# A hybrid decoder trunk on one Trainium2 core: per-head decay sums from one product per head, and three lists reordered

## The reference

```python
acs = jnp.cumsum((dt * a_neg).reshape(bsz, nc, L, ng, ne), axis=2)
ah = jnp.transpose(acs, (0, 1, 3, 4, 2))
decay = jnp.exp(jnp.where(causal, ah[..., :, None] - ah[..., None, :], -jnp.inf))
cb = jnp.einsum('bctgn,bcsgn->bcgts', cc, bc)
y_intra = jnp.einsum('bcgts,bcgets,bcsgep->bctgep', cb, decay.astype(x.dtype), xw)
w_end = jnp.exp(ah[..., -1:] - ah).astype(x.dtype)
st_loc = jnp.einsum('bcges,bcsgn,bcsgep->bcgepn', w_end, bc, xw)
y_inter = (jnp.einsum('bctgn,bcgepn->bctgep', cc, s_start.astype(x.dtype))
           * jnp.exp(acs)[..., None].astype(x.dtype))
```

## Time and profile before

| what | value |
|---|---|
| median of 3 executions | 1561.26 us (1561.2 to 1562.8) |
| profiled execution, its own time | 1561.38 us |
| its span in the trace | 1559.6 us |
| TensorE busy | 1538.0 us, 99% |
| VectorE busy | 1073.6 us, 69% |
| ScalarE busy | 809.2 us, 52% |
| GpSimd busy | 153.5 us, 10% |
| granted TensorE clock | 0.999 of full |
| HBM traffic | 173 GB/s over the span |

### The profile page before, as it was taken

How to read it: one execution, slowest core, us unless ns; L and a number is a source line. 1 busy time by engine, 2 the same in 40 slices (tenths; PEclk the granted TensorE clock), 3 DMA queues, 4 the chain that set the end, 5 groups by cost and what they waited for, 6 DMA issues and landing times.

```text
span 1559.6 us, 28133 instructions
## 1 busy us (share of the span) xinstructions
PE 1538.0 (99%) x11594; PEld 1439.7 (92%) x11594; DVE 1073.6 (69%) x1314; ACT 809.2 (52%) x1141; POOL 153.5 (10%) x147
## 2 busy tenths in 40 slices
PE   7999999999999999999999999999999999999998
PEld 6999999999999979999899999998999999799996
DVE  5556578889887546565765556799888866555556
ACT  6444385664655355443564445755766633544444
POOL 1000011233130000000000000113243100000001
PEclk9999999999999999999999999999999999999999
DMA  8665554456455556655565555454544465466551
GB/s 253 195 198 192 175 158 110 146 153 186 135 157 190 193 168 204 200 188 190 166 192 192 194 196 165 123 156 136 188 134 152 153 206 197 149 211 195 199 189 69
DMA packets 245089, 271.09 MB, mean 174 GB/s; under 512 B 12560, under 2 KB 226152, under 8 KB 245012
## 3 DMA queue, kind: packets, MB, share of 16 engines
q1 hardware_dynamic: 239504, 266.90, 53.6%
q10 hardware_dynamic: 5364, 2.98, 0.7%
q0 software_dynamic: 144, 0.15, 0.0%
HBM read 268.94 MB, written 1.05 MB: 173 GB/s over the span
## 4 chain that ended last, share of the span: by engine, by line
PE 90%; DVE 4%; issue 3%; ACT 2%; DMA 1%; SPq 0%; POOL 0%; ACTq 0%; POOLq 0%; DVEq 0%
PE bank L1562 29%; PE bank L1646 28%; PE bank L1592 8%; PE bank L1593 8%; PE bank L1594 8%; PE bank L1995 1%; PE bank L1587 1%; PE bank L1850 1%; DVE w_lo L936 1%; PE bank L1578 1%; PE bank L1580 1%; PE bank L1579 1%; ACT w_hi L530 1%; DVE xcv L1174 1%; DMA w_raw<-in_w_ffn_dram 1%
## 5 line engine op out<-in xcount | busy, mean ns | idle before, releaser
L936 DVE TENSOR_TENSOR w_lo<-w_raw,w_hi 128x2048 fp32r<-128x2048 f32 x248 | 576.9, 2328 | 315.8 <-ACT w_hi L530 315.5
L530 ACT ACTIVATE w_hi<-w_raw 128x2048 fp32r<-128x2048 f32 x248 | 474.1, 1916 | 307.4 <-PE bank L1646 131.0
L1646 PE MATMUL bank<-f_lo,w_hi 128*128 128x256 f32 x1280 | 355.6, 278 | 0.0
L1646 PE MATMUL bank<-f_hi,w_lo 128*128 128x256 f32 x1280 | 353.5, 276 | 0.0
L1646 PE MATMUL bank<-f_hi,w_hi 128*128 128x256 f32 x1240 | 342.6, 276 | 0.0
L1562 PE MATMUL bank<-u_hi,w_hi 128*128 128x256 f32 x1152 | 326.6, 283 | 1.3 <-DVE w_lo L936 1.3
L1562 PE MATMUL bank<-u_lo,w_hi 128*128 128x256 f32 x1152 | 319.9, 278 | 0.0
L1562 PE MATMUL bank<-u_hi,w_lo 128*128 128x256 f32 x1152 | 319.9, 278 | 0.0
L1646 PEld LDWEIGHTS bank<-f_hi,w_lo 128*128 128x128 f32 x1280 | 240.4, 188 | 0.0
L1646 PEld LDWEIGHTS bank<-f_lo,w_hi 128*128 128x128 f32 x1280 | 240.4, 188 | 0.0
L1646 PEld LDWEIGHTS bank<-f_hi,w_hi 128*128 128x128 f32 x1240 | 232.8, 188 | 0.0
(11 more groups left out here) (308 smaller groups left out, 2453.8 us busy)
## 6 DMA issues: line engine op xcount, KB each, us to landing
w_raw<-in_w_ffn_dram SPq DMA_DIRECT2D x262, 512.0 KB, 4.3
w_raw<-in_w_in_dram SPq DMA_DIRECT2D x160, 512.0 KB, 4.9
w_raw<-in_w_branch_b_dram SPq DMA_DIRECT2D x32, 512.0 KB, 4.4
w_raw<-in_w_branch_a_dram SPq DMA_DIRECT2D x16, 512.0 KB, 4.5
w_raw<-in_w_out_dram SPq DMA_DIRECT2D x16, 512.0 KB, 4.1
w_raw<-in_w_ple_gate_dram SPq DMA_DIRECT2D x16, 512.0 KB, 4.3
y_feat<-in_w_ple_dram ACTq DMA_DIRECT2D x2, 1024.0 KB, 4.9
h<-in_x_dram SPq DMA_DIRECT2D x2, 512.0 KB, 5.5
```

The lines of the kernel that those rows point to most:

```text
L530: a_.activation(whi[slot][:, :, :], raw[slot][:, :, :], ACT.Copy).then_inc(sem["w_hi"], 1)
L936: v_.tensor_tensor(wlo[slot][:, :, :], raw[slot][:, :, :], whi[slot][:, :, :].bitcast(F32), ALU.subtract).then_inc(sem["w_lo"], 1)
L1646: i = mm(o, four(w[slot])[:, k, cs], x[:, rows0 + k, :], start=opens, stop=(not start and k == 3 and q == 2), skip_group_check=True)
```

## The change

Once a layer, when dA is there, VectorE writes its hi and lo parts into `twin`, zeroed matrices with 40 columns per chunk and group that hold the group's 8 heads twice, at columns 0 and 32. TensorE multiplies them with the triangle `tri_le_r`: 16 products of 40 by 128, so that the running sums acs of every head stand as rows, twice, in partitions 0 to 7 and 32 to 39 of banks 4 and 5. ScalarE copies them rounded into the tile `acs` (`sums_high`), VectorE replaces rows 32 to 39 by what the rounding left (`sums_low`). Another product gives acs as columns (`acol`). `segments` and `from_start` are gone. A head's row is put on all partitions by one product of 128 by 256 with `pick`, a matrix that has ones in the two rows of that head (`sums(half)`, four products, twice a group). ScalarE then takes, per head and chunk, Relu(acol - row) and the exponential of minus that, four heads and two chunks at once, and the exponential of the row for cs. The building of R_hi and R_lo is gone. POOL clears `acs` and `twin` and makes `pick` once a layer. The order of VectorE's list changes at several places too, in group 0 and in the loop, and ScalarE's with it.

```diff
+                g_.memset(acs[:, :, :].bitcast(F32), 0.0)
...
+                    i = g_.memset(twin[b][:, :, :, :].bitcast(F32), 0.0)
...
+                    i = g_.tensor_tensor(pick[b][:, :, :], ident[:, e].unsqueeze(2).broadcast_to([P, EH // 2, P]),
+                                         ident[:, f].unsqueeze(2).broadcast_to([P, EH // 2, P]), ALU.add)
...
-                    def distances_of(g, c, half):
-                        part_of(R_hi, dA_hi, g, c, half)
-                        part_of(R_lo, dA_lo, g, c, half).then_inc(sem["r_built"], 1)
+                    def sums_high():
+
+                        act.wait_ge(sem["acs_done"], lay + 1)
+                        for b in range(2):
+                            i = a_.activation(acs[0:40, 2 * b:2 * b + 2, :],
+                                              bank[4 + b][0:40, :].rearrange("p (g s) -> p g s", g=2), ACT.Copy)
+                        i.then_inc(sem["acs_hi"], 1)
...
+                    def decay(half):
+
+                        act.wait_ge(sem["seg_done"], G * 2 + (half + 1))
+                        for e in range(4 * half, 4 * half + 4):
+                            for c in range(NC):
+                                i = a_.activation(seg[:, c, e, :], bank[4 + e // 2][:, (e % 2) * S + c * P:(e % 2) * S + (c + 1) * P],
+                                                  ACT.Relu, scale=-1.0, bias=acol[:, c, bass.ds(g * EH + e, 1)])
+                        i.then_inc(sem["gap_ready"], 1)
+                        for e in range(4 * half, 4 * half + 4, 2):
+                            a_.activation(cs[:, e:e + 2, :], two(4 + e // 2)[:, :, P:2 * P], ACT.Exp)
+                        act.wait_ge(sem["gap_ready"], G * 2 + (half + 1))
+                        a_.activation(seg[:, :, 4 * half:4 * half + 4, :], seg[:, :, 4 * half:4 * half + 4, :],
+                                      ACT.Exp, scale=-1.0).then_inc(sem["exp_done"], 1)
...
+                pe.wait_ge(sem["dA_split"], lay + 1)
+                for g in range(NG):
+                    for c in range(NC):
+                        o = bank[4 + g // 2][0:40, (g % 2) * S + c * P:(g % 2) * S + (c + 1) * P]
+                        mm(o, twin[0][:, c, g, :], tri_le_r[:, :], start=True, stop=False)
+                        i = mm(o, twin[1][:, c, g, :], tri_le_r[:, :], start=False, stop=True)
+                i.then_inc(sem["acs_done"], 1)
...
-                    def segments(c, half):
...
-                    def from_start():
...
+                        for e in range(4):
+                            i = mm(bank[4 + 2 * half + e // 2][:, (e % 2) * S:(e % 2 + 1) * S], pick[half][:, e, :],
+                                   acs[:, bass.ds(g, 1), :].rearrange("p a b -> p (a b)"), start=True, stop=True)
+                        i.then_inc(sem["seg_done"], 1)
...
-                        conv(2, 0, (4, 5), xcv[:, 2:4, :])
-                        silu(2, xcv[:, 2:4, :])
-                        mask_cb()
+                        conv(2, 0, (4, 5), xcv[:, 2:4, :])
+                        mask_cb()
+                        silu(2, xcv[:, 2:4, :])
```

More of the change, by code:

```diff
@@ L112, in trunk @@
         top[0] = place(feat_at, 512, 1024)
+        ha_hi_at = top[0]
         ha_hi = sb("ha_hi", [P, 2 * MH, S], F32R)
+        ha_lo_at = top[0]
         ha_lo = sb("ha_lo", [P, 2 * MH, S], F32R)
+        last_group = 2 * (MH - 1) * S * 4
+        pick = [at(f"pick{b}", [P, EH // 2, P], F32R, off + last_group)[0] for b, off in enumerate((ha_hi_at, ha_lo_at))]
         top[0] = place(top[0], 512, 1024)
@@ L186, in trunk @@
         late = a
-        xwe_at = late + NC * EH * HP * 4
+        twin = [at(f"twin{b}", [P, NC, NG, 40], F32R, late + b * 40 * NC * NG * 4)[0] for b in range(2)]
         xw, a = at("xw", [P, NC, EH * HP], F32, a)
@@ L800, in body @@
                         step(9)
[L801 to L805, removed]
-                        act.wait_ge(sem["y_done"], G + 1)
-                        for half in range(2):
-                            part_of(R_lo, dA_lo, g + 1, 0, half).then_inc(sem["r_built"], 1)
                     act.wait_ge(sem["ha32_ready"], G + 1)
@@ L1108, in softplus_gates, with sums_low @@
                 dve.wait_ge(sem["dA_ready"], lay + 1)
-                ch.add(v_.tensor_copy(dA_hi[:, :, :], dA[:, :, :]))
+                dve.wait_ge(sem["twin_clear"], lay + 1)
+                by_group = dA[:, :, :].rearrange("p c (g e) -> p c g e", g=NG)
+                for r in (0, 32):
+                    ch.add(v_.tensor_copy(twin[0][:, :, :, r:r + EH], by_group))
                 ch.wait()
-                v_.tensor_tensor(dA_lo[:, :, :], dA[:, :, :], dA_hi[:, :, :].bitcast(F32), ALU.subtract)\
-                    .then_inc(sem["dA_split"], 1)
+                for r in (0, 32):
+                    i = v_.tensor_tensor(twin[1][:, :, :, r:r + EH], by_group, twin[0][:, :, :, r:r + EH].bitcast(F32),
+                                         ALU.subtract)
+                i.then_inc(sem["dA_split"], 1)
+            def sums_low(lay):
+                dve.wait_ge(sem["acs_hi"], lay + 1)
+                for b in range(2):
+                    o = acs[32:40, 2 * b:2 * b + 2, :]
+                    i = v_.tensor_tensor(o, bank[4 + b][32:40, :].rearrange("p (g s) -> p g s", g=2), o.bitcast(F32),
+                                         ALU.subtract)
+                i.then_inc(sem["acs_ready"], 1)
             def gate_rows(lay):
@@ L1290, in body @@
                         gate_rows(lay)
+                        sums_low(lay)
                         step(3)
@@ L1880, in body @@
                         pe.wait_ge(sem["tok_ready"], lay * 2 + 2)
-                        segments(1, 0)
-                        segments(1, 1)
-                        unit(Z0, lambda *a: feat(*a, between=from_start))
+                        sums(0)
+                        unit(Z0, lambda *a: feat(*a, between=lambda: sums(1)))
                         cb()
@@ L1899, in body @@
                         unit(BC, feat)
-                        unit(QK, lambda *a: feat(*a, between=lambda: segments(0, 0)))
-                        segments(0, 1)
-                        unit(X01, lambda *a: feat(*a, between=lambda: segments(1, 0)))
-                        segments(1, 1)
+                        unit(QK, lambda *a: feat(*a, between=lambda: sums(0)))
+                        unit(X01, lambda *a: feat(*a, between=lambda: sums(1)))
                         evac(QK)
@@ L1906, in body @@
                         unit(X23, feat)
-                        unit(V, lambda *a: tok(*a, between=from_start))
+                        unit(V, tok)
                         cb()
```

107 lines of the change are left out of this document (47 added, 60 removed).

## The result

The changed kernel takes **1580.86 us** (median of four, 1578.81 to 1581.81) against 1561.47 for the kernel before (four runs): a ratio of 1.012, 95% interval 1.0105 to 1.0135. It is slower by 19.4 us. I had said 1570 with a range up to 1574: the side was right, the size less than half of what came. The profiled execution took 1580.18 us, its span is 1578.4, and the granted clock is 0.994 of full, against 0.999 before.

A forecast was written before the change was run, and what follows sets the result against it. TensorE was busy all the time, VectorE's loop list within 1% of it. With w_lo late, 61.4 us a group puts Z1 of group 3 4.3 us later, 8.6 over two layers: 1561.3 + 8.6 = 1569.9, said 1570; range 1553 to 1574.

The forecast's parts named there:

- Products, 12.8 us: TensorE, per layer: old products worth 22.3 us go, new ones cost 7.4 and 2.1; ends 10.9 and 14.9.
- ScalarE: A decay takes 3.7 us, costing nothing in the loop; in group 0 silu(1) starts at 247.5 instead of 246.94.
- Group 0: End of group 0 on VectorE: hrms stands behind a w_lo, so L1362 starts at 276.0, 2.1 us later.
- C: End of the third convolution's last step in a group, on VectorE; in group 1 forecast 1.6 us later, at 306.7.
- VectorE's own period, 59.8 us: VectorE's time per loop group, 60.9 us before, less 1.1 us from moving w_lo and the mask earlier.
- The port: Loop, SBUF access: POOL's seg starts before silu(2), which is slowed; the w_lo of Z1 ends at C + 7.7.
- The sum: Loop groups take 61.4 us: 33.3, 10.3, 10.05 and 7.8; Z1 of group 3 comes 4.3 us later per layer.
- Z1's start to the end of the next QK: TensorE stretch of the loop, first term of the group time: 32.3 us before, forecast 33.3.
- the two rings: Loop dependency chain from Z1's start through QK, convolutions and w_lo to the next Z1, forecast at 61.4 us per group.
- TensorE stays the bound: Rival: all 12.8 us of saved products come through, perhaps 1.4 us of waits too; 1547 to 1550 us, chance 0.12.
- VectorE gets the port for silu(2) and the w_lo: Rival: VectorE runs both in one go, Z1 of group 3 comes 3.0 us earlier; 1555 us, chance 0.18.
- The race of the third: Rival: silu(2) starts before POOL's first seg, but the w_lo stands behind that seg; 1559.5 us, chance 0.20.

The follow-up runs named there:

- experiments 1: Changed kernel with silu(2) put back ahead of mask_cb in the loop: 1561.45 us, ratio 0.9994 to the kernel before.
- experiment 5: Changed kernel with silu(2) back ahead of mask_cb and the old end of group 0 in VectorE's list: 1557.72 us, ratio 0.9975.
- experiment 7: Changed kernel with VectorE's list in the old order everywhere, keeping the new sums and ScalarE's changed order: 1556.09 us, ratio 0.9966.
- experiment 2: Changed kernel, mask still ahead of silu(2), but GpSimd's first seg step waits for that silu: 1558.76 us, ratio 0.9978.
- experiment 4: Changed kernel with 20 extra 256-column products on TensorE ahead of Z1 in groups 1 to 3 of each layer: 1573.84 us, ratio 1.0075.
- number 10: Changed kernel with VectorE's old order except mask_cb ahead of silu(2), and GpSimd held until that silu is done: 1554.04 us, ratio 0.9949.
- experiment 9: Changed kernel with GpSimd's first seg step held until silu(2) is done and the old end of group 0: 1555.46 us, ratio 0.996.
- experiment 8: Kernel before with one edit, mask_cb ahead of silu(2) in the loop: 1586.35 us, ratio 1.0161.
- experiment 6: Changed kernel with the loop order silu(2), w_lo of Z1, mask_cb, and the old end of group 0: 1567.12 us, ratio 1.0031.

## Why the prediction came out wrong

**Products, 12.8 us.** The twin products take what I gave them, about 0.06 us each; TensorE's timeline of the changed kernel:

```profile
224.02 0.22 PE L1771 MATMUL bank<-tri_le_r,twin 128*40 128x128 f32 x1
224.08 0.22 PE L1772 MATMUL bank<-tri_le_r,twin 128*40 128x128 f32 x1
```

The Trainium skill (TensorE: Matmul & The Clock Gate, Back-to-back issue gap) has about 81 ns for a steady product of 128 columns; here, with 40 columns of weights, it is 60. Comparing the starts of TensorE's units in the two traces, a loop group is shorter by 1.6 us over the units BC to V, where I had 1.86, and group 0 by 0.9 and 1.0. That makes 11.5 us in all; by the distances between the starts of the old and the new products alone it is 12.5. Both are between my ends of 10.9 and 14.9. Right.

**ScalarE.** silu(1) of group 0 at 247.05; I had 247.5, and a decay at 3.7 (the first of group 0 runs from 237.17 to 240.83). Right.

**Group 0.** L1373 at 275.55, forecast 276.0; hrms behind the w_lo, as said. Right, and the price too: C of group 1 at 306.22, forecast 306.7. Not seen: TensorE itself waits 2.1 us there for gate_a. Here that is swallowed by the later wait for w_lo; it shows once that one is gone (experiments 1 and 5).

**VectorE's own period, 59.8 us.** Not confirmed. With the port out of the way (experiment 5) Z1 comes after 59.7 and 59.8 us in the first layer, but TensorE has no wait there from Z1 of group 1 to Z1 of group 3, so this is TensorE's own pace: the 61.3 us from group 2 to group 3 before, in which it did not wait either, less the 1.6 us of products. That the number is mine is luck; it shows only that VectorE needs no more. And the mask, whose early place was 0.35 us of my sum, stands late in that run. The old order has 60.4 and 60.5 (experiment 7) and is not slower: what the moves gain per group they lose once in group 1, whose Z1 starts at 310.54 in experiment 5 and at 309.04 in experiment 7.

**The port.** POOL first, silu 2.6 (2.73), the w_lo of Z1 done at C + 7.7 (7.8), Z1 of group 1 at 314.5 (314.14). Right in every step, and experiment 2 shows it as the cause. The trace agrees once more with the exclusive lock of the Trainium skill (SBUF — State Buffer, Who interferes with whom).

**The sum: the step that failed.** "61.4 us per group". In the changed kernel it took 64.8 and 63.8 from one Z1 to the next. The failed term is its first, "Z1's start to the end of the next QK", which I took from the trace before and so at Z1's old pace: what a lower clock behind the new wait costs was put at nothing. VectorE's rows on the way from Z1 of group 1 to Z1 of group 2:

```profile
349.90 0.42 DVE L1230 SCALAR_TENSOR_TENSOR qT<-bank,rB 128x256 f32<-128x256 f32 x1 [1.11 <-PE bank L1572]
...
357.97 2.29 DVE L933 TENSOR_TENSOR w_lo<-w_raw,w_hi 128x2048 fp32r<-128x2048 f32 x1 [0.39 <-ACT w_hi L540]
...
360.90 0.74 DVE L1182 TENSOR_SCALAR xcv<-xin,gcw,gcb 128x256 f32<-128x256 f32 x2
...
368.25 2.71 DVE L1185 SCALAR_TENSOR_TENSOR xcv<-xin,gcw,xcv 128x256 f32<-128x256 f32 x6
```

From Z1 at 314.14 to the evacuation of QK at 349.90 it is 35.76 us where I had 33.3. Z1 itself is 2.4 longer than the 5.5 of before, and that is the difference. From there to the convolution of X01 it is 11.00 instead of 10.3, for hand-overs that I had left out (0.39 ahead of the w_lo at 357.97, for its w_hi). Then 10.06 to C, as forecast, and C + 7.96. From group 2 to group 3 the first two are 34.82 (Z1 1.65 longer) and 11.07. So Z1 of group 3 came at 442.75 instead of 437.3. Of the 5.8 us that the two rings were longer than forecast, about 4 are Z1's slow products, 3.6 of them the clock's if one counts from the 5.75 us of an undisturbed Z1 behind a wait; the rest are mostly the hand-overs. The first layer lost 9.8 us and the second 9.0, where I had 4.3 each: in the second the clock fell behind the waits of groups 1 and 3 only, and the slow Z1 of group 3 comes on top. That the clock is a cause and no companion is experiment 4's finding; the share of the hand-overs is read from the trace and was not tried.

**The rivals.** "TensorE stays the bound" (1547 to 1550) did not come with the port free either: experiment 7, which is clear of the port's trouble, gains 5.6 us, and the best, number 10, 7.7. From Z1 of group 1 to Z1 of group 3 TensorE does hold the pace in experiment 5, without a wait; but a wait of 2.26 us is left ahead of that stretch, and number 10 has waits of 1.1 and 1.0 us around group 1. "VectorE gets the port for silu(2) and the w_lo" (1555) is nearly experiment 2 and 9: 1558.76 and 1555.46. Its price was near, but nothing grants that turn unless GpSimd is made to wait. The race of the third (1559.5) was lost: GpSimd started 0.2 us ahead of silu(2). The range left out what lies above 1574 because I thought that a late w_lo costs the wait and no more.

## What to carry to other kernels

Before a signal is given earlier, list all who start on it. Here the mask releases two: ScalarE, which should have it early, and GpSimd, whose SBUF steps then stand in the way of VectorE; a wait on GpSimd alone parts the two and is worth more than either order. And cost a new wait of 2 us or more on TensorE at the wait plus a unit's products at a lower clock: here that was about two thirds on top (2.2 behind 3.3, 1.4 behind 2.26) where the clock fell, behind four waits of six.

## What was not expected of the hardware

The granted clock fell in or behind waits of 1.9 to 4.5 us in the mixers (1.94 in experiment 8, 4.47 in experiment 6): to a mean of 0.69 and 0.79 over the following 8 us in the changed kernel, and to 0.56 over 3.9 us in experiment 5, where two products took 0.86 instead of 0.43 us. Behind a wait of 0.94 (experiment 9) it did not fall. It is not the same each time: of two waits of 2.09 us at the same place one was followed by 1.00, the other by 0.79, and in the changed kernel it stayed full behind the wait of 2.24 us in group 3. And useless products in the wait gave back 7.0 us of 19.4.
